# Twelve-product FFN pairs in fp32r: the 48-column shift moves from the weights to the operands they meet

## The reference

```
x = x + 0.5 * swiglu(rmsnorm(x), ffn1)          # gate|up 1024 -> 2 x 2816, down 2816 -> 1024
x = x + token_mixing(rmsnorm(x))                # HGRN2 heads and a short convolution
x = x + cross_attention(rmsnorm(x), rmsnorm(mem))
x = x + 0.5 * swiglu(rmsnorm(x), ffn2)
return rmsnorm(x)
```

## Time and profile before

| | |
|---|---|
| median of 3 runs | 1114.1 us (1113.47 to 1114.87) |
| the profiled execution | 1113.43 us |
| its span, first to last instruction | 1111.6 us |
| PE busy | 1100.8 us, 99% |
| DVE / ACT / POOL busy | 633.8 / 527.4 / 437.1 us |
| weight loads (PEld), beside PE | 972.6 us, 87% |

### The profile page before, as it was taken

How to read it: one execution, slowest core, us unless ns; L and a number is a source line. 1 busy time by engine, 2 the same in 40 slices (tenths; PEclk the granted TensorE clock), 3 DMA queues, 4 the chain that set the end, 5 groups by cost and what they waited for, 6 DMA issues and landing times.

```text
span 1111.6 us, 17495 instructions
## 1 busy us (share of the span) xinstructions
PE 1100.8 (99%) x6434; PEld 972.6 (87%) x6434; DVE 633.8 (57%) x923; ACT 527.4 (47%) x735; POOL 437.1 (39%) x545
## 2 busy tenths in 40 slices
PE   9999999999999999999999999999999999999997
PEld 8889999988888888888888888888899999988886
DVE  7887777442222668888668133466977777440012
ACT  6455555542324555654366443354555555542221
POOL 0000000486665544434548883163000000485651
PEclk9999999999999999999999999999999999999999
DMA  7287675332333221222313442122676675332312
GB/s 241 79 229 184 179 198 170 115 112 97 113 100 108 76 77 57 76 76 77 114 57 127 158 170 76 39 77 76 180 199 180 170 196 170 115 114 96 112 57 76
DMA packets 49458, 136.89 MB, mean 123 GB/s; under 512 B 4736, under 2 KB 11008, under 8 KB 49280
## 3 DMA queue, kind: packets, MB, share of 16 engines
q1 hardware_dynamic: 43888, 118.90, 30.7%
q0 software_dynamic: 4320, 15.73, 8.2%
q10 hardware_dynamic: 1200, 1.57, 0.4%
HBM read 134.09 MB, written 2.10 MB: 123 GB/s over the span
## 4 chain that ended last, share of the span: by engine, by line
PE 53%; POOL 25%; issue 21%; DVE 0%; POOLq 0%; ACT 0%; DVEq 0%
POOL wl L465 25%; PE bank L1497 8%; PE bank L1499 8%; PE bank L1498 8%; PE bank L1606 4%; PE bank L1604 4%; PE bank L1605 4%; PE score L1606 3%; PE score L1604 3%; PE score L1605 3%; PE o_bank L1606 1%; PE o_bank L1605 1%; PE o_bank L1604 1%; PE bank L1561 1%; PE bank L1569 0%
## 5 line engine op out<-in xcount | busy, mean ns | idle before, releaser
L465 POOL TENSOR_TENSOR wl<-raw,wh 128x256 fp32r<-128x256 f32 x511 | 410.9, 837 | 324.7 <-ACT wh L507 281.3
L507 ACT ACTIVATE wh<-raw 128x1024 fp32r<-128x1024 f32 (+1 forms) x120 | 125.6, 1052 | 148.1 <-PE bank L1499 144.0
L1497 PE MATMUL bank<-xh,wh 128*128 128x512 f32 x456 | 182.2, 400 | 0.0
L1499 PE MATMUL bank<-xh,wl 128*128 128x512 f32 x456 | 177.8, 390 | 0.0
L1498 PE MATMUL bank<-xl,wh 128*128 128x512 f32 x456 | 177.7, 390 | 0.0
L479 POOL DMA_DIRECT2D raw<-w_all x30 | 26.1, 868 | 324.8 <-DMA raw<-w_all 324.8
L1497 PE MATMUL bank<-zr,wh 128*128 128x512 f32 (+1 forms) x374 | 140.8, 377 | 0.0
L1499 PE MATMUL bank<-zr,wl 128*128 128x512 f32 (+1 forms) x374 | 140.7, 376 | 0.0
L1498 PE MATMUL bank<-zr,wh 128*128 128x512 f32 (+1 forms) x374 | 140.7, 376 | 0.0
L950 DVE SCALAR_TENSOR_TENSOR x<-bank,x 128x512 f32<-128x512 f32 (+1 forms) x31 | 21.3, 686 | 173.0 <-PE bank L1499 173.0
L1498 PEld LDWEIGHTS bank<-xl,wh 128*128 128x128 f32 x456 | 85.7, 188 | 18.7 <-issue 1.7
(11 more groups left out here) (304 smaller groups left out, 2586.9 us busy)
## 6 DMA issues: line engine op xcount, KB each, us to landing
raw<-w_all SPq DMA_DIRECT2D x200, 512.0 KB, 3.3
raw<-w_all POOLq DMA_DIRECT2D x30, 512.0 KB, 5.2
zf<-w_all SPq DMA_DIRECT2D x30, 256.0 KB, 4.4
x<-x_t SPq DMA_DIRECT2D x8, 256.0 KB, 6.1
out_t<-x SPq DMA_DIRECT2D x8, 256.0 KB, 2.5
raw<-w_all SPq DMA_DIRECT2D x6, 256.0 KB, 6.1
memf<-mem_t ACTq DMA_DIRECT2D x1, 1024.0 KB, 4.7
raw<-w_all ACTq DMA_DIRECT2D x2, 256.0 KB, 3.9
```

The source lines that it names most:

```text
L465: ins = nc.gpsimd.tensor_tensor(l[:, slot, two], raw[:, slot, two], h[:, slot, two].bitcast(f32), SUB)
L507: nc.scalar.activation(unit_hi(u)[:, 0:wide], raw[:, slot, 0:wide], ACT.Copy).then_inc(hi_ready, 1)
L1497: nc.tensor.matmul(out_, a[0], b_[0], start=first, stop=False)
L1499: return nc.tensor.matmul(out_, a[1], b_[0], start=False, stop=last)
```

## The change

All weights, sums and held blocks go back to multiples of 512, and the moving operands of the pairs go up by 48 columns. In detail:

- `wh` and `wl` are plain tensors at multiples of 512; `for_256`, `unit_hi`, `unit_lo`, `wpair_256`, the `nearer` wait and the filler go. `held` is at multiples.
- `xh_both` and `xl_both` have 48 columns more. `xh`, `xl` (column 0) serve x by gain; `xh_apart`, `xl_apart` (column 48) hold the x made anew, both for the pairs and for the eight groups of 512 columns on it in each FFN (`src=made`). `t_h`, `t_l`, `t_f` stand 48 columns further.
- A step of `x_split` reaches 48 columns into the next block of the old x, so it waits for one block more (`x_old` +3 for +2).
- The last output's half products use plain `wh`, `wl` against plain hidden tiles.
- ACT makes the hi part of unit `P_UNIT + 2` inside the last pair, before the copy of `p5`, and no longer behind the pair. POOL's last four units go through the loop, 16 pieces for 15, and ACT's copy of the first of them has 1024 columns for 768.
- Small tensors are placed elsewhere; `rstd`, `acc`, `sq`, `gbuf`, `ubuf`, `ident` and `masks` end up 192 bytes above multiples of 512, `ones` stays at a multiple.

| matmuls | how many | offset before | offset after |
|---|---|---|---|
| 256 columns, pairs | 30 x 84 = 2520 | 192 | 192 |
| 512 columns on the x made anew | 16 x 24 = 384 | 0 | 192 |
| 256 columns, last output | 132 | 192 | 0 |
| all others in fp32r | | 0 | 0 |

```diff
-        wh_both = sb("wh", [128, APART + SLOTS * UNIT], f32r)
...
-        wl_both = sb("wl", [128, APART + SLOTS * UNIT], f32r)
...
-        wh, wl = slots(wh_both, APART), slots(wl_both, APART)
-        wh_apart, wl_apart = slots(wh_both, 0), slots(wl_both, 0)
...
-        xh = sb("xh", [128, KC, T], f32r)
-        xl = sb("xl", [128, KC, T], f32r)
+        wh = sb("wh", [128, SLOTS, UNIT], f32r)
+        wl = sb("wl", [128, SLOTS, UNIT], f32r)
...
+        xh_both = sb("xh", [128, KC * T + APART], f32r)
...
+        xl_both = sb("xl", [128, KC * T + APART], f32r)
...
+        xh, xl = at_column(xh_both, 0), at_column(xl_both, 0)
+        xh_apart, xl_apart = at_column(xh_both, APART), at_column(xl_both, APART)
...
         def held(z, first, n=1):
-            return z[:, first * T + 128 - APART:(first + n) * T + 128 - APART]
+            return z[:, first * T + 128:(first + n) * T + 128]
...
-        def by_k(ap):
-            return ap.rearrange("p (k t) -> p k t", k=4)
+        def by_k(z, first):
+            return z[:, first * T + APART:(first + 2) * T + APART].rearrange("p (k t) -> p k t", k=4)
...
-            whole(U_FFN2 + P_UNIT, NU - SLOTS)
-            for u in range(NU - SLOTS, NU):
...
+            whole(U_FFN2 + P_UNIT, NU)
...
-                nearer = for_256(u + 1 - SLOTS) and not for_256(u)
-                wide = 128 * DOWN_SPLIT[-1] if u == NU - SLOTS else UNIT
-                act.wait_ge(unit_used, u + 1 - SLOTS + nearer)
-                nc.scalar.activation(unit_hi(u)[:, 0:wide], raw[:, slot, 0:wide], ACT.Copy).then_inc(hi_ready, 1)
+                act.wait_ge(unit_used, u + 1 - SLOTS)
+                nc.scalar.activation(wh[:, slot, :], raw[:, slot, :], ACT.Copy).then_inc(hi_ready, 1)
...
-                        act.wait_ge(x_old, (KC - 1) * which + 2 * i + 2)
+                        act.wait_ge(x_old, (KC - 1) * which + 2 * i + 3)
...
-                    nc.scalar.activation(xh[:, 2 * i:2 * i + 2, :], xn[:, 2 * i:2 * i + 2, :], ACT.Copy).then_inc(xn_hi, 1)
+                    nc.scalar.activation(xh_apart[:, 2 * i:2 * i + 2, :], xn[:, 2 * i:2 * i + 2, :], ACT.Copy).then_inc(xn_hi, 1)
...
+                    else:
+                        ahead(us)
                     act.wait_ge(r5_done, n + 1)
...
-                ahead(up - 2)
                 ahead(up - 1)
...
+                made = xh_apart, xl_apart
                 for c in range(2 * old, 2 * pre):
-                    group(u0 + c, g0 + c, ready=(xn_lo, KC * which) if c == 2 * old else None)
+                    group(u0 + c, g0 + c, src=made, ready=(xn_lo, KC * which) if c == 2 * old else None)
...
-                lower, upper = (xh[:, 0:4, :], xl[:, 0:4, :]), (xh[:, 4:8, :], xl[:, 4:8, :])
+                lower, upper = (xh_apart[:, 0:4, :], xl_apart[:, 0:4, :]), (xh_apart[:, 4:8, :], xl_apart[:, 4:8, :])
...
-                            last = product(bank[(gd + KC - 1 + h) % 4][:, HALVES[h]], wpair_256(u % SLOTS, 128 * k, 128 * k + 128),
+                            last = product(bank[(gd + KC - 1 + h) % 4][:, HALVES[h]], wpair(u % SLOTS, 128 * k, 128 * k + 128),
```

More of the change, by code:

```diff
@@ L120, in block_kernel, with at_column @@
         raw = sb("raw", [128, SLOTS, UNIT])
+        wh = sb("wh", [128, SLOTS, UNIT], f32r)
+        wl = sb("wl", [128, SLOTS, UNIT], f32r)
+        x = sb("x", [128, KC, T])
+        xh_both = sb("xh", [128, KC * T + APART], f32r)
         par = sb("par", [128, NPAR])
-        wh_both = sb("wh", [128, APART + SLOTS * UNIT], f32r)
[L123 to L126, removed]
-        wl_both = sb("wl", [128, APART + SLOTS * UNIT], f32r)
-        def slots(z, first):
-            return z[:, first:first + SLOTS * UNIT].rearrange("p (s n) -> p s n", s=SLOTS)
-        wh, wl = slots(wh_both, APART), slots(wl_both, APART)
-        wh_apart, wl_apart = slots(wh_both, 0), slots(wl_both, 0)
[L135 to L146, removed]
-        xh = sb("xh", [128, KC, T], f32r)
-        xl = sb("xl", [128, KC, T], f32r)
+        ones = sb("ones", [128, 128])
+        xl_both = sb("xl", [128, KC * T + APART], f32r)
+        def at_column(z, first):
+            return z[:, first:first + KC * T].rearrange("p (k t) -> p k t", k=KC)
+        xh, xl = at_column(xh_both, 0), at_column(xl_both, 0)
+        xh_apart, xl_apart = at_column(xh_both, APART), at_column(xl_both, APART)
         rstd = sb("rstd", [128, T])
@@ L155, in block_kernel @@
         half_tanh = gbuf[:, 0, :]
-        ones = sb("ones", [128, 128])
         ident = sb("ident", [128, 128])
         masks = sb("masks", [128, MASK_COLS], u8)
-        sb("room_zf", [128, 112])
+        lbs = sb("lbs", [128, 8, HEADS])
+        few = sb("few", [128, 2])
         eps, one = few[:, 0:1], few[:, 1:2]
+        cols = sb("cols", [128, TT])
+        sb("room_zf", [128, 16])
         ffn_mem = ExitStack()
@@ L172, in held @@
         def held(z, first, n=1):
-            return z[:, first * T + 128 - APART:(first + n) * T + 128 - APART]
+            return z[:, first * T + 128:(first + n) * T + 128]
         def hidden(z, first, n=1):
             return z[:, HID_AT + first * T:HID_AT + (first + n) * T]
-        def by_k(ap):
-            return ap.rearrange("p (k t) -> p k t", k=4)
-        t_h = [by_k(tiles(zr, 2 * o, 2)) for o in range(4)]
-        t_l = [by_k(tiles(zr, 8 + 2 * o, 2)) for o in range(4)]
-        t_f = [by_k(tiles(zf, 8 + 2 * o, 2)) for o in range(4)]
+        def by_k(z, first):
+            return z[:, first * T + APART:(first + 2) * T + APART].rearrange("p (k t) -> p k t", k=4)
+        t_h = [by_k(zr, 2 * o) for o in range(4)]
+        t_l = [by_k(zr, 8 + 2 * o) for o in range(4)]
+        t_f = [by_k(zf, 8 + 2 * o) for o in range(4)]
         sum_h, sum_l = held(zr, 16, 2), held(zr, 18, 2)
@@ L461, in _, with lo @@
         def _(pool):
-            def lo(slot, h=wh, l=wl, pieces=KC):
-                for k in range(0, pieces, 2):
+            def lo(slot):
+                for k in range(0, KC, 2):
                     two = slice(128 * k, 128 * k + 256)
-                    ins = nc.gpsimd.tensor_tensor(l[:, slot, two], raw[:, slot, two], h[:, slot, two].bitcast(f32), SUB)
+                    ins = nc.gpsimd.tensor_tensor(wl[:, slot, two], raw[:, slot, two], wh[:, slot, two].bitcast(f32), SUB)
                 ins.then_inc(lo_ready, 1)
@@ L519, in ahead_loop @@
                 act.wait_ge(unit_used, i4 + (u + 1 - SLOTS))
-                nc.scalar.activation(unit_hi(u), raw[:, slot, :], ACT.Copy).then_inc(hi_ready, 1)
+                nc.scalar.activation(wh[:, slot, :], raw[:, slot, :], ACT.Copy).then_inc(hi_ready, 1)
             def square(src, n):
@@ L600, in g2_split @@
                     act.wait_ge(unit_used, used)
-                    nc.scalar.activation(wh_apart[:, slot, :], raw[:, slot, :], ACT.Copy).then_inc(hi_ready, 1)
+                    nc.scalar.activation(wh[:, slot, :], raw[:, slot, :], ACT.Copy).then_inc(hi_ready, 1)
                 def pair(j, i=None):
@@ L987, in x_low @@
                     two = slice(2 * i, 2 * i + 2)
-                    V_.tensor_tensor(xl[:, two, :], xn[:, two, :], xh[:, two, :].bitcast(f32), SUB).then_inc(xn_lo, 2)
+                    V_.tensor_tensor(xl_apart[:, two, :], xn[:, two, :], xh_apart[:, two, :].bitcast(f32), SUB).then_inc(xn_lo, 2)
                 B11, B12, B21, B22 = xn[:, 0:4, 0:Q], xn[:, 0:4, Q:T], xn[:, 4:8, 0:Q], xn[:, 4:8, Q:T]
@@ L1621, in first_product @@
                         pe.wait_ge(group_read, g0 + 2 * pre + 4)
-                    seven(E_bank[p], (wh_apart[:, 2 * p, :], wl_apart[:, 2 * p, :]), 0, lower, left, True).then_inc(r1_done, 1)
+                    seven(E_bank[p], (wh[:, 2 * p, :], wl[:, 2 * p, :]), 0, lower, left, True).then_inc(r1_done, 1)
                 def pair(j, i=None):
@@ L1627, in pair @@
                     n, u = (n0 + j, 0) if i is None else (i * 2 + (n0 + j), i * 4)
[L1628 to L1629 removed]
+                    g1 = wh[:, 2 * p, :], wl[:, 2 * p, :]
+                    g2 = wh[:, 2 * p + 1, :], wl[:, 2 * p + 1, :]
                     g3 = sum_h, sum_l
@@ L1646, in pair @@
                     else:
-                        group(u0 + P_UNIT, g0 + P_UNIT)
+                        group(u0 + P_UNIT, g0 + P_UNIT, src=made)
                     pe.wait_ge(t_lo, 4 * which + 4)
@@ L1659, in ffn @@
                 for c in range(P_UNIT + 1, N_UP):
-                    group(u0 + c, g0 + c)
+                    group(u0 + c, g0 + c, src=made)
                 ud, gd, nd = u0 + N_UP, g0 + N_UP, len(DOWN_SPLIT)
```

9 lines of the change are left out of this document (1 added, 8 removed).

## The result

The changed kernel takes 1105.61 us (median of 4 runs, 1105.33 to 1106.13) against 1113.84 us for the kernel before on the same chip (4 runs, 1113.47 to 1114.87): a ratio of 0.9925, interval 0.9908 to 0.9942. It is 0.75% **faster**, by 8.2 us. The profiled execution took 1106.13 us, its span 1104.3 us.

A forecast was written before the change was run, and what follows sets the result against it. PE was taken as the bound, by the distance between matmul starts. Pairs 0, 512-column groups 0.12 and last output 0.5 summed to +0.6 us: 1114.0, or 1114.7 us in terms of the median; range 1113.3 to 1120.5.

The forecast's parts named there:

- Pairs, 2520 products: 256-column pairs in the FFNs: offset stays 192, so cost 0, with bounds of -11.1 and +5.3 us.
- Rival 3: Pairs fall into the better pace through a new entry state: -10.5 us, 1103.6 us; chance 0.17.
- I take the floor: 384 products of 512 columns on the x made anew: stay at 226.7 ns, only settling, 0.12 us.
- rival 1: 512-column products at offset 192 do not settle: 4.4 to 8.3 ns each, 1116.4 to 1117.9 us; chance 0.22.
- Last output: Its 132 products go from offset 192 to 0 and slow down: +0.5 us together, at best 0.
- Waits: Later x_split steps keep 0.7 of 1.3 us cover; moved ACT and POOL work delays nothing: no cost.
- Rival 2: Pairs run at the worse pace, 2520 x 2.1 = +5.3 us, in all +5.9, 1120.0 us; chance 0.09.
- Rival 4: Operand places have no effect and the paces differ for another reason: 1114.1 us; chance 0.07.

The follow-up runs named there:

- e1: Kernel before with one small float32 product, and its wait, ahead of the pairs of each FFN; nothing moved: 1103.18 us against 1113.84, ratio 0.9911.
- e6: e3 with one more 512-column product in the last group ahead of the pairs of each FFN, plus a wait: 1104.51 us, ratio 0.9918.
- e7: Changed kernel with a small float32 product ahead of the groups on the x made anew and one more 512-column product ahead of the pairs: 1119.42 us.
- e8: Kernel before with one more 512-column product, at offset 0, in the last group ahead of the pairs, plus a wait: 1114.47 us, ratio 1.0008.
- e3: Kernel before with the weights of the four 512-column groups ahead of the pairs moved, so these run at offset 192: 1115.07 us, ratio 1.0009.
- e5: e3 with a filler that puts every operand behind raw 192 bytes further: 1115.38 us in a single execution.
- s64: Kernel before with APART 64 for 48, so pairs and last output run at offset 256 bytes: 1119.78 us, ratio 1.0049.
- e9: e1 with cross-attention's eight K groups at offset 192 and small products ahead of them and of the last output: 1102.34 us, ratio 0.9900.

## Why the prediction was wrong

- **"Pairs, 2520 products ... I take 0, since offset is all that distinguishes rows 5 from rows 3"** is the step that failed. The price of a product at offset 192 has two values, and I had read both (117.8, and 113.4 behind the sum of squares). I took it that the pairs keep the one that they had, as both stages held theirs for hundreds of products. They hold it, but it is set on entry. e1 shows this with the operands in place, e6 and e7 with one product in either direction. The term was taken at 0 and measured -11.2 us, which is its lower bound, 2520 x -4.4.
- **Rival 3** named this mechanism and its reason, "the state in which the pairs begin", at 0.17. The argument against it was that the entries from 512 columns had all given 117.8. But all of these came out of groups at offset 0, and e8 shows that there one product more makes no difference either. The change took such an entry away. That alone was not enough, since e3 and e5 did the same and kept 117.8: that the changed kernel's entry is a good one could not be worked out from the rows, and for the change it is luck. Its 1103.6 us was 2.0 too low, because of the next point.
- **"I take the floor"** for the 384 products is the second step that failed. They don't settle at offset 192: 233.3 ns, 6.6 above 226.7, within the bounds of 0 and 8.3, +2.5 us for the 0.1 in the sum. The reason given, that a 512-column product has the time of 256 columns to spare, does not hold at this offset, as e3 shows too, where only the weights' place differs from the kernel before and 96 products keep 233.3 ns to the last. This was **rival 1**, which I took with the pairs unchanged; the two are not exclusive, and I had not put them together. Together they are 1103.6 + 2.5 - 0.12, 1106.0 us, against 1105.6 measured.
- **Last output**, +0.5 predicted, +0.5 measured, at 119.9 as the earlier trace rows had it. **Waits**: none new but the 0.2 us on `qb`, `x_split` keeps the 0.7 us of cover that was worked out, and POOL's end costs nothing.
- **Rival 2** (the worse pace, 119.9) did not come. **Rival 4**, nothing has an effect, is refuted, too: s64 differs from the kernel before by the pairs' and last output's offset and the places of a few small tensors, and is 5.8 us slower, with 120.0 ns for 117.8 in the pairs. The rule of the Trainium skill behind it is that PE, with two independent read ports, never waits on anyone ("SBUF — State Buffer", Who interferes with whom). Read as in the prediction, that no operand's place costs PE anything, it does not describe these runs: 113.3 to 120.0 ns by the place and the entry. That it is the two ports that hold each other up is not shown.
- **The range** left rival 3 out at 0.17 and rested on the pairs' pace being a property of the stage. With a price known to have two values at the same offset, and a change that alters what precedes the stretch, both values belonged in it.

What stays open: what in the chip tells the two states apart. The runs show which step comes last ahead of the pairs, not what is stored in between. The changed kernel itself enters from a pattern that e3 and e5 didn't have (steps of 233, 233 and 234 ns, no alternation) and gets the better pace; why its groups fall into that pattern, when e5's operands have the same places modulo 512, was not settled. Nor was the changed kernel run with one product more and nothing else: that its pace, too, turns on the entry is shown by e7 alone, where the small float32 product had first made its groups alternate.

## What to carry to other kernels

Before a long stretch of equal matmuls is called bound by TensorE, divide it by their number, and look for the same instruction at another pace elsewhere in the trace. If there is one, try a single small product ahead of the stretch before moving any data: here one of some 0.2 us in each FFN brought 10.7 us, where the whole rearrangement brought 8.2. When an operand moves, price the steady pace and the way in separately, and let the range hold every pace that the trace shows for that offset. And after any edit to what precedes such a stretch, even one of no cost in itself, read its pace again: it may have turned.

## What the runs showed of the hardware

- The same 256-column fp32r product, moving operand 192 bytes above the stationary one, has two steady paces, 113.3 and 117.8 ns. At offsets 0 and 256 it has 119.8 to 120.0; at 128 and 384 it has 120.0, and 118.6 behind a sum of squares. At 192 a pace held for 1332 products on end once entered.
- 512-column products take 226.7 ns at offset 0 and 233.3 at 192, steady, in two patterns with the same mean. The better place for 256 columns is the worse for 512, which is why e1 beats the changed kernel.
- Where the 512-column products ahead alternate between 231 and 236 ns, one of them more exchanges the two paces of the whole stretch behind (e6, e7); where they run evenly at offset 0, it does not (e8). A sum of squares between made the exchange in both directions (e9).
- With the granted clock at 0.50 for some 3 us, 512-column steps took 0.43 us for 0.23 (e7), 1.6 us in all; such a stretch can pass for an effect of the edit.
